# Adding the expert rows into x2 in DRAM: weights applied at the evacuation, scatters that accumulate

## The reference

```python
x = x + g1 * token_mixer(...)                 # the kernel calls this x2
h = modulate(rmsnorm(x, norm_ffn_g), sh2, sc2)
# router: two experts for each token, their weights w sum to 1
y = zeros
for e in range(16):
    a = silu(h @ w_gate[e]) * (h @ w_up[e])
    y = y + comb[:, e:e+1] * (a @ w_down[e])  # comb is w where e was chosen, else 0
x = x + g2 * y
return rmsnorm(x, final_norm_g)
```

## Time and profile before

| | |
|---|---|
| median of three runs | 976.4 us |
| the profiled execution | 974.74 us, of which the span is 972.9 us |
| PE busy | 864.5 us, 89% of the span |
| DVE, ACT, GpSimd busy | 516.0, 202.5, 233.6 us |
| mean granted TensorE clock | 0.934 |
| DMA over the whole run | 198.44 MB, mean 204 GB/s |
| last expert matmul to the end of the span | about 28 us |

### The profile page before, as it was taken

One profiled execution on the slowest core, in us unless ns is written; L12 is line 12 of the kernel. 1 busy time (PEld: TensorE's weight loads), 2 busy tenths in 40 slices (PEclk: granted clock), 3 DMA queues, 4 the chain that ended last, 5 costly groups with the idle time before them and its releaser, 6 DMA issues.

```text
span 972.9 us, 13521 instructions
## 1 busy us (share of the span) xinstructions
PE 864.5 (89%) x5284; PEld 646.5 (66%) x5284; DVE 516.0 (53%) x702; ACT 202.5 (21%) x252; POOL 233.6 (24%) x227
## 2 busy tenths in 40 slices
PE   4699999999999999987999798649999979999970
PEld 2678889988789878766888598535555534555530
DVE  1953597998598974868899546421111101111116
ACT  2142211122422124621223242201000000000012
POOL 0440131221532210143443322011222212222220
PEclk9579999999999999988999899759999989999995
DMA  9722221121221121137776847469997999999716
GB/s 305 248 87 93 94 97 63 47 84 60 71 88 44 44 87 44 43 123 250 235 249 198 280 158 279 175 256 389 398 379 273 392 398 393 392 372 394 273 44 259
DMA packets 123516, 198.44 MB, mean 204 GB/s; under 512 B 10551, under 2 KB 72263, under 8 KB 123473
## 3 DMA queue, kind: packets, MB, share of 16 engines
q1 hardware_dynamic: 101826, 167.43, 48.2%
q10 hardware_dynamic: 17616, 19.40, 6.1%
q0 software_dynamic: 4032, 11.03, 3.1%
HBM read 189.44 MB, written 10.49 MB: 205 GB/s over the span
## 4 chain that ended last, share of the span: by engine, by line
PE 69%; DVE 13%; DMA 6%; SPq 5%; issue 3%; ACT 2%; POOL 1%; ACTq 0%; DVEq 0%; POOLq 0%
PE proj L740 14%; PE proj L513 11%; PE proj L515 11%; PE proj L514 11%; PE ha L776 7%; SPq L429 5%; PE pp L566 4%; DVE ada_acc L1276 3%; DMA ada_p<-in_w_ada 2%; DVE osq L1252 2%; DMA ew<-in_w_down 2%; PE pp L730 1%; DMA xt_t<-in_xT 1%; PE pp L521 1%; PE ha L627 1%
## 5 line engine op out<-in xcount | busy, mean ns | idle before, releaser
L740 PE MATMUL proj<-ew,heT 128*64 128x256 f32 x1536 | 178.7, 386 | 8.3 <-DMA ew<-in_w_gate 6.0
L740 PEld LDWEIGHTS proj<-ew,heT 128*64 128x64 f32 x1536 | 109.3, 139 | 76.6 <-issue 19.0
L513 PE MATMUL proj<-h_hi,w_hi 128*128 128x512 f32 x384 | 153.9, 401 | 4.4 <-DVE h_lo L1068 2.1
L515 PE MATMUL proj<-h_hi,w_lo 128*128 128x512 f32 x384 | 150.4, 392 | 0.0
L514 PE MATMUL proj<-h_lo,w_hi 128*128 128x512 f32 x384 | 150.3, 391 | 0.0
L1581 POOL TENSOR_TENSOR w_lo<-w_raw,w_hi 128x2048 fp32r<-128x2048 f32 x15 | 72.0, 4802 | 101.8 <-ACT w_hi L824 101.8
L776 PE MATMUL ha<-ew,aT 128*64 128x512 f32 x384 | 88.1, 599 | 3.4 <-DMA ew<-in_w_down 2.4
L824 ACT ACTIVATE w_hi<-w_raw 128x2048 fp32r<-128x2048 f32 x38 | 72.5, 1908 | 88.1 <-PE proj L515 35.0
L1181 DVE SCALAR_TENSOR_TENSOR acc<-u_t,cols_t,acc 128x512 f32<-128x512 f32 x120 | 87.8, 792 | 0.0
L513 PEld LDWEIGHTS proj<-h_hi,w_hi 128*128 128x128 f32 x384 | 72.7, 189 | 21.3 <-DVE w_lo L1046 3.9
L515 PEld LDWEIGHTS proj<-h_hi,w_lo 128*128 128x128 f32 x384 | 72.7, 189 | 15.6
(11 more groups left out here) (221 smaller groups left out, 1340.8 us busy)
## 6 DMA issues: line engine op xcount, KB each, us to landing
ew<-in_w_gate SPq DMA_DIRECT2D x34, 1024.0 KB, 12.3
ew<-in_w_up SPq DMA_DIRECT2D x34, 1024.0 KB, 11.9
ew<-in_w_down SPq DMA_DIRECT2D x34, 1024.0 KB, 14.0
w_raw<-in_w_in SPq DMA_DIRECT2D x28, 1024.0 KB, 5.1
ada_p<-in_w_ada ACTq DMA_DIRECT2D x32, 512.0 KB, 4.8
ada_w<-in_w_ada SPq DMA_DIRECT2D x8, 1024.0 KB, 12.1
w_raw<-in_w_o_hgrn SPq DMA_DIRECT2D x4, 1024.0 KB, 5.6
w_raw<-in_w_out SPq DMA_DIRECT2D x4, 1024.0 KB, 6.1
```

The lines of the kernel that those rows point to most:

```text
L513: pe.matmul(outap, a_hi, b_hi, start=first, stop=False)
L515: return pe.matmul(outap, a_lo, b_hi, start=False, stop=last)
L740: mm = pe.matmul(out_ps[JS * i:JS * i + JS, 0:FG], heT[:, c_, JS * j_:JS * j_ + JS], w[:, k, FG * i:FG * i + FG], start=(kb == 0), stop=(k ...
```

## The change

The expert row is scaled by its pair's weight when it is evacuated, and scattered with addition into a DRAM row that already holds x2. `job1` gets a second half that holds each pair's weight, so the same matmul (66 columns for 33) also gives the weight of each slot (`wslot`). The multiplication by the pair's number moves from `slot1` to `job1`. ACT writes x2 (2 MB) to rows 0 to 511 of `y_dram` once it has copied the first job's tokens. `y_out` multiplies by the slot's weight and the g2 rows in one instruction. Empty slots now go to spare rows behind the first 512, so all 128 parts of each scatter are written. The end loads one row for each token, and DVE's two weighted sums there are gone.

```diff
-        fin = [at("fin0", "HT", [P, 2, D]), ...]
+        fin = [at(f"fin{i}", "HT", [P, D], F32, 8192 * i) for i in range(TT)]
+        fo = [at(f"fo{i}", "HT", [P, D], F32, 8192 * i + 4096) for i in range(TT)]
-        job1 = at("job1", "MASK", [P, 2 * TT, NPOS])
+        job1 = at("job1", "MASK", [P, 2 * TT, 2, NPOS])
@@ SP, the end
-                sp.dma_start(fin[tt][:, :, :], y_dram.rearrange("(c a p) d -> a p c d", c=2, p=P)[tt]).then_inc(s_fl[tt], 16)
+                sp.dma_start(fin[tt][:, :], y_dram[P * tt:P * (tt + 1), :]).then_inc(s_fl[tt], 16)
@@ PE, the index table
-                mm = pe.matmul(pp[:, 704:704 + NPOS], slot1[:, c, :], job1[:, c, :], ...)
+                mm = pe.matmul(pp[:, 704:704 + 2 * NPOS], slot1[:, c, :], job1[:, c, :, :].rearrange("p a j -> p (a j)"), ...)
@@ ACT
             tokens_out(0, True)
+            act.wait_ge(s_x2d, 8)
+            act.dma_start(y_dram[0:T, :].rearrange("(a p) d -> p a d", p=P), x2_t[:, :, :]).then_inc(s_xw, 16)
...
-                act.wait_ge(s_f2, tt + 1)
+                act.wait_ge(s_fl[tt], 16)
-                act.activation(fsq[:, :], fin[tt][:, 1, :], ACT.Square, ...)
+                act.activation(fsq[:, :], fin[tt][:, :], ACT.Square, ...)
@@ DVE, routing
-                                  r(18, c, c + 1), con_t[:, K_VAL + c:K_VAL + c + 1],
-                                  ALU.is_equal, ALU.mult).then_inc(s_oh1, 1)
+                                  r(18, c, c + 1), None, ALU.is_equal).then_inc(s_oh1, 1)
...
+            tt_(job1[:, :, 1, :], job1[:, :, 0, :], col(wsel[:, :, :].rearrange("p a b -> p (a b)")).broadcast_to([P, 2 * TT, NPOS]), ALU.mult)
+            settle()
+            tt_(job1[:, :, 0, :], job1[:, :, 0, :], col(con_t[:, K_VAL:K_VAL + 2 * TT]).broadcast_to([P, 2 * TT, NPOS]), ALU.mult)
             settle()
             dve.memset(nst[:, 0:1], 0.0).then_inc(s_oj, 1)
...
-            go(dve.tensor_scalar(rt[:, 10, 0:NPOS], table, 0.0, float(PADIDX), ALU.is_equal, ALU.mult))
-            go(dve.scalar_tensor_tensor(rt[:, 11, 0:NPOS], ...))
+            go(dve.scalar_tensor_tensor(idx_s[:, :], table, float(GT), ...))
+            go(dve.tensor_scalar(rt[:, 10, 0:NPOS], table, 0.0, con_t[:, K_VAL + TT:K_VAL + TT + 1], ALU.is_equal, ALU.mult))
             settle()
-            tt_(idx_s[:, :], rt[:, 10, 0:NPOS], rt[:, 11, 0:NPOS], ALU.add)
-            settle()
             dve.tensor_single_scalar(idx_g[:, :], idx_s[:, :], GT * T - 1, ALU.bitwise_and).then_inc(s_ig, 1)
+            dve.wait_ge(s_ig, 1)
+            dve.tensor_tensor(idx_s[:, :], idx_g[:, :], rt[:, 10, 0:NPOS], ALU.add).then_inc(s_wj, 1)
+            dve.tensor_copy(wslot[:, :], pp[:, 704 + NPOS:704 + 2 * NPOS]).then_inc(s_wj, 1)
@@ DVE, y_out
-                dve.tensor_tensor(y_sb[:, :], ha[:, 1, 0:DG_], rows[:, 3, 0:DG_], ALU.mult).then_inc(s_y, 1)
+                dve.scalar_tensor_tensor(y_sb[:, :], ha[:, 1, 0:DG_], wslot[:, bass.ds(at_, 1)], rows[:, 3, 0:DG_],
+                                         ALU.mult, ALU.mult).then_inc(s_y, 1)
@@ DVE, the end (both weighted sums, L1531 and L1534, removed)
+            for tt in range(TT):
+                inv = nst[:, 4 + tt:5 + tt]
+                dve.wait_ge(s_fa, 2 * tt + 2)
+                dve.reciprocal(inv, inv).then_inc(s_fr, 1)
+                dve.wait_ge(s_fr, tt + 1)
+                dve.wait_ge(s_fl[tt], 16)
+                dve.scalar_tensor_tensor(fo[tt][:, :], fin[tt][:, :], inv, gfin[:, :], ALU.mult, ALU.mult).then_inc(s_fo, 1)
@@ GpSimd
-                                        bounds_check=GT * NPAIR - 1, oob_is_err=False).then_inc(s_ys, 16)
+                                        compute_op=ALU.add).then_inc(s_ys, 16)
...
+            pool.wait_ge(s_wj, 2)
             for s in range(LANES):
+                if s == 1:
+                    pool.wait_ge(s_xw, 16)
```

More of the change, by code:

```diff
@@ L60 @@
 NPAIR = 2 * T
-PADIDX = 1 << 14
 ROUND = 1.5 * 2.0 ** 23
@@ L127, in trunk_kernel @@
                      ("ON0", 16384), ("COLS", 4 * C_ALL), ("CONST", 4 * K_ALL),
-                     ("MASK", 4 * NLEV * 64), ("TMP", 4096), ("RST", 2048), ("SMALL", 1024),
+                     ("MASK", max(4 * NLEV * 64, 16 * TT * NPOS)), ("TMP", 4096), ("RST", 2048), ("SMALL", 1024),
                      ("TABLE", 3 * TBL)):
@@ L192, in trunk_kernel @@
         part = at("part", "SMALL", [P, 1], F32, 320)
+        wslot = at("wslot", "SMALL", [P, NPOS], F32, 512)
         rb_t = at("rb_t", "SMALL", [P, NE], F32, 768)
@@ L208, in trunk_kernel @@
         gfin = at("gfin", "TMP", [P, D])
-        fin = [at("fin0", "HT", [P, 2, D]), at("fin1", "HT", [P, 2, D], F32, 8192),
-               at("fin2", "HT", [P, 2, D], F32, 16384), at("fin3", "HT", [P, 2, D], F32, 24576)]
+        fin = [at(f"fin{i}", "HT", [P, D], F32, 8192 * i) for i in range(TT)]
+        fo = [at(f"fo{i}", "HT", [P, D], F32, 8192 * i + 4096) for i in range(TT)]
         fsq = at("fsq", "ST", [P, D])
@@ L333, in trunk_kernel @@
         s_gl = sem("final_gain_loaded")
-        s_f1 = sem("final_first_added")
-        s_f2 = sem("final_second_added")
+        s_xw = sem("x2_rows_written")
+        s_wj = sem("slot_weights_copied")
         s_fr = sem("final_root_inverted")
@@ L501, in _ @@
             for tt in range(TT):
-                sp.dma_start(fin[tt][:, :, :], y_dram.rearrange("(c a p) d -> a p c d", c=2, p=P)[tt]).then_inc(s_fl[tt], 16)
+                sp.dma_start(fin[tt][:, :], y_dram[P * tt:P * (tt + 1), :]).then_inc(s_fl[tt], 16)
             for tt in range(TT):
                 sp.wait_ge(s_fo, tt + 1)
-                sp.dma_start(out[P * tt:P * (tt + 1), :], fin[tt][:, 0, :]).then_inc(s_out, 16)
+                sp.dma_start(out[P * tt:P * (tt + 1), :], fo[tt][:, :]).then_inc(s_out, 16)
             sp.wait_ge(s_out, 16 * TT)
@@ L718, in _ @@
             for c in range(2 * TT):
-                mm = pe.matmul(pp[:, 704:704 + NPOS], slot1[:, c, :], job1[:, c, :], start=(c == 0), stop=(c == 2 * TT - 1))
+                mm = pe.matmul(pp[:, 704:704 + 2 * NPOS], slot1[:, c, :], job1[:, c, :, :].rearrange("p a j -> p (a j)"),
+                               start=(c == 0), stop=(c == 2 * TT - 1))
             mm.then_inc(s_ix, 1)
@@ L998, in _ @@
             for tt in range(TT):
-                act.wait_ge(s_f2, tt + 1)
+                act.wait_ge(s_fl[tt], 16)
                 if tt:
                     act.wait_ge(s_fa, 2 * tt - 1)
-                act.activation(fsq[:, :], fin[tt][:, 1, :], ACT.Square, accum_out=nst[:, tt:tt + 1]).then_inc(s_fa, 1)
+                act.activation(fsq[:, :], fin[tt][:, :], ACT.Square, accum_out=nst[:, tt:tt + 1]).then_inc(s_fa, 1)
                 act.wait_ge(s_fa, 2 * tt + 1)
@@ L1460, in _ @@
             settle()
-            tt_(job1[:, :, :], ids.rearrange("p (o j) -> p o j", o=1).broadcast_to([P, 2 * TT, NPOS]),
+            tt_(job1[:, :, 0, :], ids.rearrange("p (o j) -> p o j", o=1).broadcast_to([P, 2 * TT, NPOS]),
                 col(r(18, 8, 16)).broadcast_to([P, 2 * TT, NPOS]), ALU.is_equal)
+            settle()
+            tt_(job1[:, :, 1, :], job1[:, :, 0, :],
+                col(wsel[:, :, :].rearrange("p a b -> p (a b)")).broadcast_to([P, 2 * TT, NPOS]), ALU.mult)
+            settle()
+            tt_(job1[:, :, 0, :], job1[:, :, 0, :], col(con_t[:, K_VAL:K_VAL + 2 * TT]).broadcast_to([P, 2 * TT, NPOS]),
+                ALU.mult)
             settle()
@@ L1479, in _ @@
             table = pp[:, 704:704 + NPOS]
-            go(dve.tensor_scalar(rt[:, 10, 0:NPOS], table, 0.0, float(PADIDX), ALU.is_equal, ALU.mult))
-            go(dve.scalar_tensor_tensor(rt[:, 11, 0:NPOS], table, float(GT), part[:, 0:1].broadcast_to([P, NPOS]),
+            go(dve.scalar_tensor_tensor(idx_s[:, :], table, float(GT), part[:, 0:1].broadcast_to([P, NPOS]),
                                         ALU.mult, ALU.add))
-            settle()
-            tt_(idx_s[:, :], rt[:, 10, 0:NPOS], rt[:, 11, 0:NPOS], ALU.add)
+            go(dve.tensor_scalar(rt[:, 10, 0:NPOS], table, 0.0, con_t[:, K_VAL + TT:K_VAL + TT + 1], ALU.is_equal, ALU.mult))
             settle()
             dve.tensor_single_scalar(idx_g[:, :], idx_s[:, :], GT * T - 1, ALU.bitwise_and).then_inc(s_ig, 1)
+            dve.wait_ge(s_ig, 1)
+            dve.tensor_tensor(idx_s[:, :], idx_g[:, :], rt[:, 10, 0:NPOS], ALU.add).then_inc(s_wj, 1)
+            dve.tensor_copy(wslot[:, :], pp[:, 704 + NPOS:704 + 2 * NPOS]).then_inc(s_wj, 1)
             for i in range(1, GT):
@@ L1503, in act_out, with y_out, lane @@
                 dve.tensor_copy(aT[:, :, :].rearrange("p c n -> p (c n)"), ha[:, 0, 0:FG]).then_inc(s_at, 1)
-            def y_out(j):
+            def y_out(j, at_):
                 dve.wait_ge(s_dn, j + 1)
                 dve.wait_ge(s_ys, j * 16 + 16)
-                dve.tensor_tensor(y_sb[:, :], ha[:, 1, 0:DG_], rows[:, 3, 0:DG_], ALU.mult).then_inc(s_y, 1)
-            def lane(j, first=False, second=False):
```

(14 more changed lines are left out.)

## The result

The changed kernel takes 983.06 us (median of five runs, 982.01 to 984.24). The ratio to the kernel before is 1.008, with a 95% interval of 1.005 to 1.011: slower by 0.8% (the two medians alone give 0.7%). The forecast was 981 us. The profiled execution takes 984.01 us, its span is 982.2 us.

What follows compares the result with a forecast made beforehand. DMA volume from 738 to 856 us was taken as the bound, with PE before and after; 974.7 + 0.9 + 11.7 + 2.1 - 9.9 = 979.5 us, forecast 981 us against the median, range 969 to 997 us.

Steps and rivals of the forecast that it cites:

- What bounds the kernel: Whole chain: PE to about 736 us, DMA volume from 738 to 856 us, PE to 944 us, then the tail.
- The final stage: End of the kernel: fewer DVE instructions and smaller loads for each tile save 9.9 us.
- ACT stays the pace: Final norm: loads come every 1.35 us, just faster than ACT's 1.5 us for each tile, so ACT sets the pace.
- The last scatters: Last two scatters: addition lengthens landing by 1.3 us and delays `y_out` by 0.8 us; together +2.1 us, bounds 0 and +5.
- The routing: Routing before the gathers: two more DVE multiplications, a wider table matmul and one step dropped; +0.9 us, all on the path.
- The scatters in the loop: Expert loop: each adding scatter costs two passes, 1.36 us; +8.3 us after 738 us and +5.1 us before.
- The overflow ahead of round 3: Before 738 us: 10.6 us of DMA work added, 7.2 us free, so 3.4 us run over into the saturated stretch.
- One pass: Rival for the loop's scatters: addition hidden inside the write, 0.68 us each; 971 us, faster; chance 0.30 (one pass or nearly).
- Four passes: Rival for the loop's scatters: engines held while the destination is fetched; 1004 us; chance 0.16 (three or more passes).
- Late landing: Rival in the expert loop: scatter landing time replaces bandwidth and holds up evacuation; at 20 us landing, 48 us; chance 0.04.
- The price at which the sign turns: Loop scatters: at about 0.95 us for each, both added terms equal 7 us and faster turns to slower.
- rival 2: The four-pass case, 1004 us, chance 0.16; against it stood an ordinary scatter under load landing 6.0 us after issue.

Runs made afterwards that it cites:

- plain_all: The changed kernel with the scatters' addition taken away, so each scatter overwrites all 128 parts; 969.92 us, ratio 0.9941 to the kernel before.
- x2_early: The changed kernel with the x2 write issued earlier, at about 617 us during routing; 976.38 us, ratio 1.0015 to the kernel before.
- add_skip: The changed kernel with empty slots skipped again while the rest still adds; 974.58 us, ratio 0.9991 to the kernel before.

## Why the prediction was right, point by point

**What bounds the kernel.** This held. The last wait for weights is still by the down product of job 15, and from there to the last but one scatter it takes 84.95 us, before 84.85. What is added to the loop acts only ahead of that point. And ahead of round 3 it is still PE that releases SP, as the chain said. PE's waits for weights from 784 us on rose from 9.3 to 15.7 us, by 6.4; 8 to 12 were foretold, and another 4.1 us came at job 6, where none were.

**The final stage.** Forecast -9.9 us, measured -9.09 (E to end). The first load lands 3.28 us after issue (967.34 to 970.62), 3.5 forecast. The chain from there was put at 7.5 us and took 8.5 (970.62 to 979.13). The step that was a little off is "ACT stays the pace": ACT's third square starts at 974.73 us after 1.27 us of waiting for its load, so the loads set the pace at one place.

**The last scatters.** Forecast +2.1, measured +3.74 us. The price of an addition was put at 1.3 us of landing and is 2.1 (4.88 against 2.77 us in plain_all); it counts in full at the last scatter. At the one before, which now also writes its empty slots, the landing grew by 2.6 us (5.05 against 2.49), and less the slack of 0.9 us that makes 1.7 where 0.8 was taken. The bounds 0 and 5 held.

**The routing.** Forecast +0.9, measured about +0.5 (from A to the start of the table matmul 32.14 us against 31.60). The two multiplications came as computed. I overlooked that dropping the second operation from `slot1` would make it cheaper. These are the rows after, and then the group of `slot1` before:

```profile
633.89 1.65 DVE L1452 TENSOR_SCALAR slot<-con_t,rt 128x128 f32<-128x128 f32 x8
...
636.69 0.43 DVE L1335 TENSOR_TENSOR job<-job,wsel 128x264 f32<-128x264 f32 x1
637.16 0.43 DVE L1335 TENSOR_TENSOR job<-job,con_t 128x264 f32<-128x264 f32 x1
...
637.86 3.65 PE L719 MATMUL pp<-job,slot 128*128 128x66 f32 x16 [7.73 <-DVE nst L1472]
```

```profile
632.61 2.13 DVE L1449 TENSOR_SCALAR slot<-con_t,rt 128x128 f32<-128x128 f32 x8
```

The eight instructions take 1.65 us with one operation and took 2.13 us with two. The 16 matmuls took 3.65 us against 3.60: 0.05 us where 0.2 was taken.

**The scatters in the loop.** Forecast +8.3 us for nine after round 3 starts, measured +6.95 (B to C). By share the price was right: 1.36 us foretold, 1.43 found. On the path it was less than by share. Of the 0.77 us that the addition costs in share, 5.5/9 = 0.61 us come through, and of the 0.51 us for empty slots 3.3/9 = 0.36. Why a fifth to a third is lost isn't settled. The two-pass rule of the Trainium skill ("Collectives: The Full Stack", The bandwidth ceiling) agrees with the trace in size: 1.43 against 0.66 us is a factor of 2.2, and the rule's own numbers give 1.9. That it is a second read which takes the time no row shows; what the rows show is 177 ns for an adding packet of 2 KB and 89 ns for a plain one.

**The overflow ahead of round 3.** Forecast 3.4 us, measured 5.7 us (after against x2_early). This is the step that was wrong in its mechanism, and its size came near by luck. "Added are 10.6 us and 7.2 us are free" put what the idle time doesn't hold on top of the saturated stretch. What happened is that the backlog reached PE: the 8 KB gate load of job 6 was issued at 710.70 us (before, at 701.32), landed 13.5 us later, and PE, which the prediction had running freely there, waited 4.12 us for it and lost 1.46 us more to the clock. That delays the down product of job 5, on whose end SP's last loads of round 2 wait. From A to this end it is 5.9 us more than before; from the end to B it is 6.46 us against 5.99 (why half a microsecond more isn't settled), and the two together are the 6.4 us of A to B. In all ten kernels the last loads of round 2 are issued 0.2 us after this product ends and B follows 6.0 to 6.6 us after it, so round 3 starts with PE and not when the DMA engines have caught up. That is also why idle time is left in spite of the backlog: the share is 0.74 in the six microseconds from 738 us and 0.59 in the four from 744 us, which against 1.05 leaves 3.5 us idle, while SP gets from its last load (738.53 us) to the next (743.94 us). I had looked at PE's waits where they were, not at how far the loads were from becoming one.

**The rivals.** One pass (971 us) is refuted by the share and by the time of a packet. Four passes (1004 us) as well. Late landing is not seen: PE never waits for an evacuation in the loop. The price at which the sign turns was summed wrongly: with the prediction's own terms both added parts make 7 us at 1.04 us for each scatter and not at 0.95, where they make 5.7. I should have shown the row for the 6.0 us of landing that rival 2 names, which the earlier trace rows doesn't hold; it is this (DMA issues of the kernel before, median us to landing last):

```profile
y_rows<-y_sb,si POOLq DMA_INDIRECT x24, 6.0
```

The terms together: -9.9, +2.1, +0.9, +8.3 and +3.4 were forecast, 4.8 us in all. Found were -9.1, +3.7, and +6.4, +7.0 for the two stretches, 8.1 us, and 1.2 us of the first 605 us that are no effect. By the medians it is +6.7 us. So the forecast missed by 2 us by the medians and by 3.3 us by the landmarks. Only the scatters in the loop were put too high (by 1.35 us); the stretch ahead of round 3, the last scatters and the final stage were put too low (by 2.1, 1.6 and 0.8 us). That the number came so near is in part luck. The ranges were also tied to the wrong prices: by the prediction's own terms 977 to 990 us is 1.6 to 2.9 passes and not 1.2 to 2.2, and 997 us is 3.5 passes.

## What to carry to other kernels

Before arithmetic is moved into a DMA, price the addition, and the parts that it must now move and didn't before, on the engines that are the bound in that stretch: here 9 us at the end were bought with 7 us in the saturated stretch, 6 us ahead of it and 4 us at the last scatters. A transfer that nobody waits for still has a place in time; put it where the DMA engines are idle (routing, here), since moving the x2 write by some 35 us gave back 6.7 us. And idle DMA time ahead of a stretch is not free as long as a load in the same queue can come late: look for the next load that the compute engine needs, however small it is, and at who releases the loads behind it.

## What was not expected of the hardware

An adding scatter of 128 parts moves them in 128 packets of 2 KB where a plain one has 64 of 4 KB, with the same bytes counted, and takes 1.43 us of the engines against 0.66, 4.88 us to land against 2.77, and 1.60 us of GpSimd's issue against 1.01. Skipped parts keep their packets: 2023 in add_skip, 2016 in the changed kernel. An 8 KB load took 13.5 us from issue to landing behind 1 MB loads of its own queue (job 6 of the changed kernel). A DVE instruction with one operation on 128 elements was some 0.06 us shorter than the same with two (8 in 1.65 us; 8 in 2.13 us before).
